# A decoder layer with product-key experts: one token block's search moved, gate tiles rounded earlier, one barrier taken out

## The chip, the cores and the metric

The kernel runs on one core of a Trainium2 chip, in one launch. The metric is the device time of that core in microseconds (us). The engines are TensorE (PE; PEld is its weight load), VectorE (DVE), ScalarE (ACT), GpSimd (POOL) and SyncE (SP). Each runs its own list of instructions in order, and they wait for each other by semaphores. DMA transfers are issued from SP's, ACT's and POOL's queues.

## The reference

One layer for 1,024 tokens of width 1,024, all in float32:

```
proj  = h @ w_in                     # attention q/k/v | recurrence f,i,q,g | memory q | 3 gates
mix   = (sum_g sigmoid(gate_g + b) * (branch_g @ w_branch_g)) @ w_out
h     = LN(alpha*h + mix)
q     = h @ w_q                      # 8 heads, 2 halves of 128
s1,i1 = top16(q1 . subkeys1); s2,i2 = top16(q2 . subkeys2)
top, pos = top16(s1 + s2 of all 256 pairs); idx = i1*128 + i2; gate = softmax(top)
out   = sum_e gate_e * gelu(h . u[idx_e]) * v[idx_e]       # 128 experts of 16,384 per token
h     = LN(alpha*h + out)
```

The three branches are a dilated sliding-window attention, a gated recurrence and a cross-attention to 256 memory tokens.

## The kernel before

Tokens go in two halves of 512 (`hf` 0 and 1), each of four blocks of 128. A half passes four stages: four heads of the branches (`PE_HEAD` and the loops over `NH`), the gated projection (`gated`, `mid_gates`, 8 steps of 6 weight tiles), the output projection with residual and norm (4 pairs of tiles) and the query projection (`query_tile`, `query`, 16 tiles). Between stages `cross(eng, n)` is a barrier: each of PE, ACT and DVE drains, adds one to `stage` and waits until all three have. SP and POOL wait on `stage` where they need it.

**Weight tiles.** A float32 product is made from three passes with rounded parts: high by high, low by high, high by low (lines 1082, 1085 and 1091). A tile of weights is rounded into `w_hi` by ACT (`weight_hi`, line 1530) and its rest is made into `w_lo` by POOL (`split_lo_only`, line 967). There are two buffers, taken in turn; `w_used` lets one be overwritten once PE has started the tile in the other. In the heads of the first half POOL makes both parts, in those of the second half both come back from DRAM. The first two gate tiles (`mid_hi(0, 0)` and `mid_hi(0, 1)`) are rounded by ACT after its last head; PE does them (`gated(0, 0)`, `gated(0, 1)`) ahead of the barrier `boundary(hf, 1)`. Behind it DVE splits the branches (lines 2306 and 2308).

**The experts of blocks 0 and 1.** In the second half DVE does expert dot products beside the layer's own work. POOL gathers rows of `u` by index into a ring of four (`u_rows`, line 988); a row's gather waits until the dot four rows back is done. The gathers stand in POOL's queue between the weight splits: in the query projection two behind each tile, 32 in all. DVE's `e_rows` (line 2089) multiplies a row by the token block and sums it; every fourth is followed by a copy (line 2093). The query projection has four groups of 8 rows; `e_gates` (line 2098) ends it.

**The searches.** A search (`topk`, lines 1971 to 2043) finds the top 16 for two expert heads of one block, so a block takes four. It needs four score matmuls of PE, and has four parts on DVE, each a chain of short instructions. Block 1 is searched beside the first half's query projection (`early_topk`, tiles named `_all`), blocks 0, 2 and 3 in the second half's heads, blocks 4 to 7 in the streamed stage (`late_topk`, tiles named `_own`).

**The streamed stage.** After the last barrier the whole table `v` passes through a ring of four tiles of 128 rows. There are nine streamed halves `p` of 64 tiles. In half `p` PE multiplies each tile with coefficients of blocks `p-1` and `p` (line 1420); from half 6, tile 32, by split parts (line 1453). Beside it DVE dots gathered `u` rows (`dot`, line 2429), a ring of seven, and in tiles 32 to 63 builds the coefficients of the next block (`hots`, `pair`). `turn(p + 1)` at tile 30 transposes the next block's indices and coefficients on PE (`transposes`, line 1099): it waits until DVE has done all dots of that block and multiplied the gates in. The next block's indices are loaded by `load_picks`. `searched(p)` says how many searches a half has, six tiles each:

```
return 3 if p < NB else 4 if p == NB else 0
```

So halves 0 to 3 have three, half 4 has four and half 5 none; NB is 4. `topk_at(p, i)` gives the search and part of a tile. Scores for a search are loaded by ACT's queue (`load_scores`: 256 KB of queries and 256 KB of keys).

## Time and profile before

| | us |
|---|---|
| median of 3 runs | 4026.82 (4024.84 to 5327.76) |
| the profiled execution | 4033.38 |
| its span, first to last instruction | 4031.1 |
| PE busy | 3658.6 (91%) |
| DVE busy | 2809.6 (70%) |
| POOL busy | 1577.5 (39%) |
| ACT busy | 1322.2 (33%) |

Busy time is the sum over an engine's instructions; a wait isn't busy. The mean granted clock of TensorE is 0.956 of full speed, and DMA moved 281 GB/s over the span. The streamed stage begins at about 1886 us. Matmul ends are modelled, so a busy PE isn't PE at its peak.

### The profile page before, as it was taken

The page shows a single profiled execution, that of the slowest core. Times are in us where ns is not written, and L with a number is a line of the kernel's source. Part 1 is how long each engine was busy: PE and PEld are TensorE (multiplying, and loading weights), DVE is VectorE, ACT ScalarE, POOL GpSimd, SP SyncE. Part 2 cuts the span into 40 slices and gives each one's busy share as a digit, 9 for nine tenths or more (in the row PEclk, how much of TensorE's full clock was granted, in tenths as well). Part 3 has the DMA queues.
Part 4 walks back from the last instruction along what each step waited for, and adds up shares of the span by engine and source line. Part 5 has one row for each costly group of instructions (what it writes and reads, how often), then busy time and mean ns, then how long its engine had stood idle before and what let it go on. Part 6 is the DMA issues. An engine that isn't in the chain of part 4 may idle for free.

```text
span 4031.1 us, 47164 instructions
## 1 busy us (share of the span) xinstructions
PE 3658.6 (91%) x14687; PEld 2513.0 (62%) x14687; DVE 2809.6 (70%) x5664; ACT 1322.2 (33%) x2671; POOL 1577.5 (39%) x1341
## 2 busy tenths in 40 slices
PE   6999989989889879868778999898998999999997
PEld 5878768777777768756534454453554545548874
DVE  1455542258778856665988888888889868868777
ACT  1333332222332332223533240330421403318445
POOL 2556534331222147656344443444544444520000
PEclk8999999989989989988899999999999999999999
DMA  7576633346767758769899999999999999984667
GB/s 242 197 237 219 218 92 99 107 149 229 237 210 240 227 167 262 265 234 335 276 400 405 393 396 368 388 387 393 389 378 369 408 401 398 393 332 143 204 213 256
DMA packets 506334, 1134.03 MB, mean 281 GB/s; under 512 B 41181, under 2 KB 250509, under 8 KB 505905
## 3 DMA queue, kind: packets, MB, share of 16 engines
q1 hardware_dynamic: 335120, 570.94, 40.7%
q0 software_dynamic: 147456, 536.94, 35.4%
q10 hardware_dynamic: 23584, 24.12, 1.7%
q8 instruction: 75, 1.23, 0.1%
q14 instruction: 99, 0.80, 0.1%
HBM read 1044.81 MB, written 89.41 MB: 281 GB/s over the span
## 4 chain that ended last, share of the span: by engine, by line
PE 33%; DVE 11%; DMA 6%; issue 2%; ACT 1%; POOL 0%; DVEq 0%; ACTq 0%
PE ps L1420 21%; PE ps L1453 6%; DVE u_ring L2429 5%; PE ps L1406 4%; DMA u_ring<-in_peer_u,pidx 4%; DMA v_ring<-in_peer_v 2%; DVE hot L2421 1%; DVE hot L2422 1%; DVE split_v L2482 1%; DMA score_in<-subkeys_t 0%; DVE got_own L2035 0%; PE h_up L1395 0%; DVE inds_own L1990 0%; DVE inds_own L1978 0%; ACT split_v L1877 0%
## 5 line engine op out<-in xcount | busy, mean ns | idle before, releaser
L1420 PE MATMUL ps<-v_ring,table 128*128 128x512 f32 x3072 | 1367.4, 596 | 19.4 <-DMA v_ring<-in_peer_v 19.2
L1023 POOL DMA_INDIRECT u_ring<-in_peer_u,pidx x800 | 775.1, 969 | 935.9 <-DVE coefe L2429 873.7
L2429 DVE CUSTOM_DVE_ANT_0 u_ring<-u_ring,h_up 128x1024 f32<-128x1024 f32 x800 | 948.0, 1217 | 138.0 <-DMA u_ring<-in_peer_u,pidx 122.1
L1420 PEld LDWEIGHTS ps<-v_ring,table 128*128 128x128 f32 x3072 | 570.1, 192 | 667.8 <-issue 632.4
L1082 PE MATMUL ps<-x_hi,w_hi 128*128 128x512 f32 x1280 | 517.0, 404 | 39.0 <-ACT w_hi L1530 23.6
L1085 PE MATMUL ps<-x_lo,w_hi 128*128 128x512 f32 x1280 | 507.1, 396 | 0.0
L1453 PE MATMUL ps<-split_v,split_c 128*128 128x512 f32 x1536 | 370.7, 395 | 20.9 <-DVE split_v L2482 18.8
L967 POOL TENSOR_TENSOR w_lo<-w_raw,w_hi 128x1024 fp32r<-128x1024 f32 x120 | 300.9, 2513 | 199.1 <-ACT w_hi L1530 193.3
L1406 PEld LDWEIGHTS ps<-hot,hot 128*128 128x128 f32 x2048 | 279.7, 201 | 150.8 <-issue 96.0
L1846 ACT ACTIVATE table<-ps 128x512 f32<-128x512 f32 (+3 forms) x256 | 230.8, 901 | 383.1 <-PE ps L1406 326.4
L1834 ACT ACTIVATE hot<-hot,by_slot 128x128 f32<-128x128 f32 x1024 | 322.0, 388 | 78.0 <-DVE hot L2421 68.3
L1453 PEld LDWEIGHTS ps<-split_v,split_c 128*128 128x128 f32 x1536 | 281.3, 188 | 97.6 <-DVE split_v L2482 35.2
L988 POOL DMA_INDIRECT e_ring<-in_peer_u,icole x224 | 229.6, 1025 | 277.1 <-DVE dotse L2089 198.6
L1406 PE MATMUL ps<-hot,hot 128*128 128x128 f32 x2048 | 289.7, 287 | 43.2 <-DVE hot L2422 18.5
L1091 PE MATMUL ps<-x_hi,w_lo 128*128 128x512 f32 x1280 | 317.3, 390 | 0.4 <-POOL w_lo L967 0.4
L1082 PEld LDWEIGHTS ps<-x_hi,w_hi 128*128 128x128 f32 x1280 | 246.3, 192 | 94.0 <-issue 13.5
L1085 PEld LDWEIGHTS ps<-x_lo,w_hi 128*128 128x128 f32 x1280 | 246.1, 192 | 52.5 <-issue 1.9
L1091 PEld LDWEIGHTS ps<-x_hi,w_lo 128*128 128x128 f32 x1280 | 239.7, 188 | 52.4 <-POOL w_lo L967 2.7
L2089 DVE CUSTOM_DVE_ANT_0 e_ring<-e_ring,h_up 128x1024 f32<-128x1024 f32 x128 | 155.0, 1220 | 130.1 <-DMA e_ring<-in_peer_u,icole 126.6
L2421 DVE TENSOR_TENSOR hot<-keys,by_slot 128x512 f32<-128x512 f32 x256 | 176.8, 691 | 96.2 <-PE ps L1406 71.4
L975 POOL TENSOR_TENSOR w_hi<-w_raw,zero 128x1024 fp32r<-128x1024 f32 x56 | 110.4, 1971 | 249.0 <-PE ps L1082 113.2
L1877 ACT ACTIVATE split_v<-v_ring 128x1024 fp32r<-128x1024 f32 x160 | 168.7, 1057 | 98.1 <-PE ps L1453 98.1
(327 smaller groups left out, 4462.5 us busy)
## 6 DMA issues: line engine op xcount, KB each, us to landing
v_ring<-in_peer_v SPq DMA_DIRECT2D x576, 512.0 KB
w_raw<-in_w_in SPq DMA_DIRECT2D x88, 512.0 KB
wh_d<-w_hi SPq DMA_DIRECT2D x56, 512.0 KB, 2.6
wl_d<-w_lo SPq DMA_DIRECT2D x56, 512.0 KB, 4.0
w_hi<-wh_d SPq DMA_DIRECT2D x56, 512.0 KB
w_lo<-wl_d SPq DMA_DIRECT2D x56, 512.0 KB
u_ring<-in_peer_u,pidx POOLq DMA_INDIRECT x800
raw_mid<-in_w_branch SPq DMA_DIRECT2D x48, 256.0 KB
```

What stands on the lines that cost most here:

```text
L967: pool.tensor_tensor(out=w_lo[b][:, 0:k, :], in0=raw[:, 0:k, :], in1=w_hi[b][:, 0:k, :].bitcast(F32), op=ALU.subtract).then_inc(w_split[b], 1)
L988: pool.indirect_dma_start(out=e_ring[:, s, :], out_offset=None, in_=u_tab, in_offset=bass.IndirectOffsetOnAxis(ap=icole[:, r, s:s + 1], ax ...
L1023: pool.indirect_dma_start(out=u_ring[:, slot_of(n, k), :], out_offset=None, in_=u_tab, in_offset=bass.IndirectOffsetOnAxis(ap=pidx[n % 2][ ...
L1082: first = pe.matmul(out, w_hi[b][:, k, :], hi[:, k, :], start=(k == 0), stop=False)
L1085: pe.matmul(out, w_hi[b][:, k, :], lo[:, k, :], start=False, stop=False)
L1091: last = pe.matmul(out, w_lo[b][:, k, :], hi[:, k, :], start=False, stop=(k == k_n - 1))
L1406: last = pe.matmul(build_bank(item)[:, P * m:P * m + P], hot2[sub % 2][:, m, :], hot1[sub % 2][:, m, :], start=True, stop=True)
L1420: last = pe.matmul(ps[2 * (n % 2) + c][:, :], table[:, row_of(n, i1), :], v_ring[:, j % V_TILES, HALF * c:HALF * c + HALF], start=(n == p ...
L1453: last = pe.matmul(ps[2 * (n % 2) + c][:, :], c_of[:, part_of(n, p, i), a, :], v[:, HALF * c:HALF * c + HALF], start=(n == p and i == 0 an ...
L1834: last = act.activation(hot1[sub % 2][:, m, :], hot1[sub % 2][:, m, :], ACT.Copy, scale=by_slot[:, 2, t0 + m:t0 + m + 1])
L1846: last = act.activation(table[:, r0:r0 + near, t0:t0 + TOK].rearrange("p i t -> p t i"), src[:, :, 0:near], ACT.Copy)
L2429: dve.tensor_tensor_reduce(out=u_ring[:, slot_of(n, k), :], in0=u_ring[:, slot_of(n, k), :], in1=h1_up[:, :, :].rearrange("p c n -> p (c n)"),
```

## The change

- ACT's head is now a function `act_head(h, last)`. The loop runs over three heads and the fourth is written out; in it `mid_hi(0, 0)` stands behind the copy `vn2` and `mid_hi(0, 1)` behind `values_out(2)`. Both halves.
- The barrier between gated and output projection is taken out in both halves. PE waits for ACT's last gates and DVE's last but one low part, and for the last only before the last high slice of the first output tile. SP loads residual and norm parameters after PE's last gated tile.
- In the second half's query projection three of block 4's four searches are done (`last_topk`), with the tiles of `early_topk`. Its loops on PE and DVE are written out, the rotated query tiles `qst_all` replace `qst`, and the keys are loaded there (1 MB).
- The streamed halves have 3, 2, 2, 2, 2, 2 searches. The last block's indices are loaded at tile 28 of half 5, not tile 48 of half 4. Some small tiles lie elsewhere.

```diff
+AHEAD = PH // 2 - 1
...
         def searched(p):
-            return 3 if p < NB else 4 if p == NB else 0
+            return 3 if p == 0 else 2 if p <= NB + 1 else 0
+
+        def first_part(p):
+            return AHEAD + sum(searched(k) for k in range(p))
...
             def load_ln(hf):
-                sp.wait_ge(stage, 3 * boundary(hf, 2))
+                sp.wait_ge(MP.sem, MP.after("B2", KD * hf + KD - 1))
...
-                    if hf == 0 and e == 2:
-                        sp.wait_ge(stage, 3 * boundary(0, 3))
+                    if e == 2:
+                        sp.wait_ge(stage, 3 * boundary(hf, 3))
                         sp.dma_start(skt_all[:, :, :], subkeys_t).then_inc(tk_in, 16)
...
-                        if p >= 1:
-                            sp.wait_ge(tk_out, late_stores(p))
...
-                        sp.wait_ge(turned, p + 2)
-                        load_picks(p + 3)
+                        if p + 3 < NBLK - 1:
+                            if p >= 1:
+                                sp.wait_ge(tk_out, late_stores(p))
+                            sp.wait_ge(turned, p + 2)
+                            load_picks(p + 3)
+                    if i == DOT_TILES and p == NB + 1:
+                        sp.wait_ge(tk_out, late_stores(NB))
+                        sp.wait_ge(turned, NBLK - 2)
+                        load_picks(NBLK - 1)
...
                 for k in range(k_n):
+                    if whole is not None and k == k_n - 1:
+                        pe.wait_ge(*whole)
...
-                cross(pe, boundary(hf, 2))
...
+                for t in range(2):
+                    pe.wait_ge(MA.sem, MA.after(f"s{t}", KD * hf + KD - 1))
+                pe.wait_ge(MV.sem, MV.after("lo", KD * hf + KD - 2))
+                out_pair(0, (MV.sem, MV.after("lo", KD * hf + KD - 1)))
+                with pe.Fori(1, KD // 2) as e:
+                    out_pair(e, None)
...
+                for q in range(PH // 2):
+                    for n in range(4):
+                        query_tile(2 * q + n // 2, n % 2)
+                        if q and n == 0:
+                            early_scores(q - 1)
...
                     spill(2)
+                    if last:
+                        mid_hi(0, 0)
                     p("p1p")
...
                     values_out(2)
+                    if last:
+                        mid_hi(0, 1)
                     v("md")
...
+                with act.Fori(0, NH - 1) as h:
+                    act_head(h, False)
+                act_head(NH - 1, True)
...
-                for t in range(2):
-                    mid_hi(0, t)
                 cross(act, boundary(hf, 1))
...
-                cross(act, boundary(hf, 2))
...
+            def last_topk(q, part):
+                topk(early, late_item(0, q), part, 4 + q % 2, late.idxu[:, 2 * TOPK * q:2 * TOPK * (q + 1)], late.gex[:, 2 * q:2 * q + 2, :])
...
-                cross(dve, boundary(hf, 2))
...
                 if hf == 1:
-                    with dve.Fori(0, PH // 2) as e:
+                    dve.wait_ge(e_out, 32)
+                    for e in range(PH // 2):
                         e_rows(0, E_PQ, G_PQ + E_PQ // E_ROWS * e, S_PQ + E_PQ * e, 0)
+                        if e:
+                            for part in range(4):
+                                last_topk(e - 1, part)
                     e_gates()
```

## Rows read from the trace of the kernel before

**Rows 1.** Timeline of PE at four stage ends: start, us, line, operation [idle before <- releaser].
```profile
541.66 0.76 PE L1082 MATMUL ps<-x_hi,w_hi 128*128 128x512 f32 x1 [7.77 <-DVE og L2130]
...
1466.34 0.77 PE L1082 MATMUL ps<-x_hi,w_hi 128*128 128x512 f32 x1 [9.75 <-ACT w_hi L1530]
...
751.37 0.54 PE L1082 MATMUL ps<-m_hi,w_hi 128*128 128x512 f32 x1 [4.36 <-ACT w_hi L1530]
...
1690.14 0.79 PE L1082 MATMUL ps<-m_hi,w_hi 128*128 128x512 f32 x1 [9.80 <-ACT w_hi L1530]
```

**Rows 2.** Windows: stretch, length, busy by engine (count), granted clock, DMA share, GB/s.
```profile
1788.00:1882.00 94.00, 89.48 (x384) 73.49 (x384) 43.66 (x73) 27.08 (x33) 70.02 (x56) 0.97 0.90 312
...
1690.00:1757.00 67.00, 55.21 (x224) 42.37 (x224) 42.56 (x74) 12.78 (x17) 49.74 (x47) 0.92 0.96 334
...
2696.00:2716.00 20.00, 20.00 (x54) 9.39 (x53) 16.80 (x60) 1.28 (x1) 5.63 (x6) 1.00 0.91 319
...
3258.00:3288.00 30.00, 30.00 (x72) 13.26 (x71) 19.54 (x33) 0.00 (x0) 14.95 (x16) 1.00 1.03 409
```

The engines stand in the order PE, PEld, DVE, ACT, POOL.

**Rows 3.** Timeline of SP and ACT in the first half's last head.
```profile
512.66 2.10 SPq L766 DMA_DIRECT2D w_raw<-in_w_in  x2
...
523.72 0.60 ACT L1587 ACTIVATE ptp<-ps 128x512 f32<-128x512 f32 x1 [2.09 <-PE ps L1099]
```

**Rows 4.** Timeline of DVE behind the barrier after the heads, both halves.
```profile
555.35 1.23 DVE L2306 CAST o_hi<-branch 128x2048 fp32r<-128x2048 f32 x1 [8.05 <-PEq L687]
...
1480.16 1.23 DVE L2306 CAST o_hi<-branch 128x2048 fp32r<-128x2048 f32 x1 [14.15 <-PEq L687]
```

**Rows 5.** Timeline of POOL and DVE around the second half's output projection.
```profile
1680.44 0.94 POOL L988 DMA_INDIRECT e_ring<-in_peer_u,icole  x1 [0.30 <-issue]
1690.17 2.38 POOL L967 TENSOR_TENSOR w_lo<-w_raw,w_hi 128x1024 fp32r<-128x1024 f32 x1 [8.79 <-ACT w_hi L1530]
...
1687.94 0.69 DVE L2337 TENSOR_TENSOR m_lo<-macc,m_hi 128x512 f32 x1
```

**Rows 6.** Groups by line, DVE, 1788 to 1882: busy, mean ns, idle before <- releasers.
```profile
L2089 DVE CUSTOM_DVE_ANT_0 e_ring<-e_ring,h_up 128x1024 f32<-128x1024 f32 x32 | 39.1, 1221 | 50.2 <-DMA e_ring<-in_peer_u,icole 49.7
```

**Rows 7.** Timeline of DVE and POOL, two searches in the first half's query projection.
```profile
901.68 0.89 DVE L1974 MAX8 vals_all<-h_up 128x8 f32<-128x128 f32 x4 [7.02 <-PE h_up L1128]
...
915.11 0.19 DVE L2039 SCALAR_TENSOR_TENSOR pidx_one<-got_all 128x32 uint32<-128x32 f32 x1
...
869.78 2.12 DVE L2039 SCALAR_TENSOR_TENSOR pidx_one<-got_all 128x32 uint32<-128x32 f32 x1
...
869.46 2.39 POOL L967 TENSOR_TENSOR w_lo<-w_raw,w_hi 128x1024 fp32r<-128x1024 f32 x1 [3.04 <-ACT w_hi L1530]
```

**Rows 8.** Timeline of DVE and POOL in the second half's query projection.
```profile
1796.40 1.22 DVE L2089 CUSTOM_DVE_ANT_0 e_ring<-e_ring,h_up 128x1024 f32<-128x1024 f32 x1 [9.88 <-DMA e_ring<-in_peer_u,icole]
...
1839.18 0.17 DVE L2093 COPY coefe<-dotse 128x4 f32 x1
...
1845.12 0.98 POOL L988 DMA_INDIRECT e_ring<-in_peer_u,icole  x1 [0.81 <-POOL icole L985]
...
1851.87 1.22 DVE L2089 CUSTOM_DVE_ANT_0 e_ring<-e_ring,h_up 128x1024 f32<-128x1024 f32 x1 [1.66 <-DMA e_ring<-in_peer_u,icole]
...
1881.75 0.29 DVE L2098 TENSOR_TENSOR coefe<-coefe,pgatee 128x128 f32<-128x128 f32 x1 [0.38 <-ACT coefe L1568]
```

**Rows 9.** Timeline of PE at the turns of streamed halves 1 to 5.
```profile
2274.48 0.38 PE L1099 MATMUL ps<-ident,key_f 128*128 128x128 f32 x2
...
2546.92 0.66 PE L1099 MATMUL ps<-ident,key_f 128*128 128x128 f32 x2 [15.11 <-DVE coefe L2434]
...
2816.25 0.66 PE L1099 MATMUL ps<-ident,key_f 128*128 128x128 f32 x2 [14.32 <-issue]
2816.70 0.42 PE L1099 MATMUL ps<-ident,coefe 128*128 128x128 f32 x1
...
3088.26 0.66 PE L1099 MATMUL ps<-ident,key_f 128*128 128x128 f32 x2 [15.95 <-issue]
...
3344.53 0.42 PE L1099 MATMUL ps<-ident,key_f 128*128 128x128 f32 x2 [3.25 <-issue]
```

More of the change, by code:

```diff
@@ L342, in layer @@
         res = at("res", [P, NB, D], offset=r_head)
[L343 to L344 removed]
+        r_top = top[0] + 8 * HALF
         ln_g = at("ln_g", [P, D], offset=r_ln)
@@ L1018, in _ @@
             pool.wait_ge(stage, 3 * boundary(1, 4))
+            for t in range(2):
+                pool.wait_ge(qp_out[t], 16 * PH * NHALF + 16)
             for n in range(1, NBLK):
@@ L1072, in _, with tile @@
             cross(pe, 1)
-            def tile(n, hi, lo, k_n, out, ready=False):
+            def tile(n, hi, lo, k_n, out, ready=False, whole=None):
                 b, m = n
@@ L1121, in early_scores @@
             def early_scores(q):
-                pe.wait_ge(tk_in, 16)
-                pe.wait_ge(QA.sem, QA.after("c1", 2 * q + 1))
+                first, block, bank = (0, 1, 6) if hf == 0 else (late_item(0, 0), 0, 4)
+                pe.wait_ge(tk_in, 16 * hf + 16)
+                pe.wait_ge(QA.sem, QA.after("c1", PH * hf + 2 * q + 1))
                 if q >= 2:
-                    pe.wait_ge(TK.sem, TK.after("rest", q - 2))
+                    pe.wait_ge(TK.sem, TK.after("rest", first + q - 2))
                 for n in range(4):
-                    last = pe.matmul(ps[6 + q % 2][:, P * n:P * n + P], qst_all[4 * (q % 2) + n][:, P:2 * P], skt_all[:, 4 * q + n, :], start=True, stop=True)
+                    last = pe.matmul(ps[bank + q % 2][:, P * n:P * n + P], qst_all[4 * (q % 2) + n][:, P * block:P * block + P], skt_all[:, 4 * q + n, :], start=True, stop=True)
                 last.then_inc(*TP.mark("s"))
@@ L1760, in mid_gates @@
                         mid_hi(j, 3 + b)
-                for t in range(2):
-                    mid_hi(0, t)
                 cross(act, boundary(hf, 1))
@@ L1793, in query @@
                     act.wait_ge(QP.sem, QP.after(f"Q{t}", it))
-                    rows = qst[t] if hf else qst_all[2 * (e % 4) + t]
-                    if hf == 0 and e >= 4:
-                        act.wait_ge(TP.sem, TP.after("s", e // 2 - 2))
+                    rows = qst_all[2 * (e % 4) + t]
+                    if e >= 4:
+                        act.wait_ge(TP.sem, TP.after("s", (late_item(0, 0) if hf else 0) + e // 2 - 2))
                     act.wait_ge(qp_out[t], 16 * it + 16)
```

50 lines of the change are left out of this document (20 added, 30 removed).

## The prediction, made before the changed kernel was run

> **What bounds the kernel now.** I read the windows first, to see which engine or transfer is full in a stretch; then the timeline where TensorE (PE) stood still; then groups by line; then single instructions. PE is busy for 91% of the span, so a part of the change pays only where PE or the end of a stage waits for it. Three places count.
>
> First, the ends of two stages in each half. After the last head PE waits 7.77 and 9.75 us for the first rounded weight tile, after the gated projection 4.36 and 9.80 us [rows 1]. Second, the second half's query projection: in 94 us VectorE (DVE) is busy 43.66, GpSimd (POOL) 70.02, DMA 0.90 of the time [rows 2]. DVE's other 50 us are waits for gathered expert rows [rows 6]. Third, the streamed stage. With no search in it PE goes from one turn to the next in 256.3 us; with three it takes 272.4 and 269.3, with four 272.0 (differences of start times in [rows 9]). DMA runs at 409 GB/s where there is no search, and at 319 where the first search holds DVE [rows 2].
>
> The sum is made against the profiled execution, 4033.4 us with a span of 4031.1; the median of the runs is 4026.8, so 6.6 lower. I take the same difference off both.
>
> **Step 1, two gate tiles rounded in the last head.** Removed: two ScalarE (ACT) roundings of 1.06 us behind the head, and the wait of PE for them. Added: the same two, earlier. The first goes where ACT waits 2.09 us for PE, here and at the same place of the second half [rows 3], so it is hidden; without that cover it would cost 1.1 us of a chain that PE follows. The second needs its buffer, which comes free as PE starts the first tile; it lies in front of ACT's wait for DVE, hidden too. POOL's two low parts move forward with them. The raw tiles are asked for 11 us before that place (512.66 against 523.72, [rows 3]), so I take them as landed. Both tiles then run from the end of the head, but the barrier behind them also waits for DVE. In the first half DVE waited 8.05 us at it and in the second 14.15 [rows 4]. The first half can thus give at most 8; there the tiles take some 10.9 us (sixteen of that kind take 89.5 us, so two 11.2, [rows 2]) after 533.9 (541.66 - 7.77, [rows 1]), so they end before DVE does: **-8**. In the second half PE needed 1480.1 - 1456.6 = 23.5 us [rows 1, 4] for a gap and two tiles, and needs 11: **-12.5**, within DVE's 14.15. Bounds: 0 and -22.
>
> **Step 2, the barrier between gated and output projection goes.** PE now starts the output tile and waits only before its last high slice for DVE's last low part. First half: 4.36 us of gap [rows 1]; the residual's load now starts with PE's last gated tile and not with the barrier, which gains a little less, so **-3.5** (0 to -4.4). Second half: it isn't PE that sets the pace (55.21 of 67 us busy, [rows 2]) but POOL, which splits a weight tile and then issues four gathers, in one queue, eight times. It had waited 8.79 us for the rounding behind the barrier [rows 5]. That wait goes; DVE's last low part ends at 1688.6, the first gather of the stage is then issued at about 1684.7 (1681.4, a split and the index copy) and lands some 7 us later, so DVE isn't late either: **-8.5** (-4, if PE's own stop for DVE counts, to -9.8).
>
> **Step 3, three searches beside the second half's query projection.** Added: 12 score matmuls on PE (12 x 0.42 us, the row at 2816.70 in [rows 9], 5 us), a 1 MB load of keys on SP's queue (some 3 us at 312 GB/s, [rows 2]), both beside the longer DVE, a wait of ACT for scores that are long made, and on DVE three searches. One ran from 901.68 to 915.4, 13.7 us, in the first half; another 15.7, since one instruction took 2.12 us and not 0.19 [rows 7]. I take 14.7. DVE's order is now: 8 rows; 8 rows, search; 8 rows, search; 8 rows, search. What is queued behind a search is the dots, and POOL waits for these: a gather into a ring of four needs the dot four rows back. POOL's splits of the weight tiles stand in the same queue, and PE waits for them.
> Worked out from the rows of before: the second group ends at 1839.35 [rows 8]. Search to 1854.1. Row 17 is dotted at 1855.4, and only then POOL can issue row 21, issued at 1845.12 before. It lands 6.75 us after its issue (1851.87 - 1845.12, [rows 8]), at 1862.2. With a split of 2.4 us [rows 7] between the pairs row 23 is issued at 1860.3 and dotted at 1867.0; the group ends at 1869.9. Search to 1884.6. Row 25 to 1885.9, row 29 issued there, the last split ends at 1890.5, row 31 issued at 1890.7, dotted at 1897.5; the group ends at 1900.2. Search to 1914.9, gate product 0.4: 1915.3, against 1882.1 [rows 8]: **+33**. PE's last tile ends at 1892.5 and isn't what is late. Nothing of the streamed stage may start, since the barrier behind it is kept.
> Lower bound: no wait of DVE but the first: from 1796.4 [rows 8], 43.7 us of rows [rows 2] and 44.1 us of searches end at 1884.2, with the gates +2.5. Upper bound: each search adds itself and a whole landing: 3 x (14.7 + 6.75) = +64. I take +33: it follows the queues row by row.
> The Trainium skill ("DMA: Bandwidth & Descriptors", Anatomy of one DMA) fits a GpSimd transfer at 2.0 us plus bytes over 436 GB/s, an estimate of 3.2 us for these 0.5 MB. The trace's 6.75 us is twice that, beside other traffic; by the rule the two exposed landings would make +26 of the +33.
>
> **Step 4, the streamed stage.** Searches per streamed half go from 3, 3, 3, 3, 4, 0 to 3, 2, 2, 2, 2, 2. Three cost (272.4 + 269.3) / 2 - 256.4 = 14.5 us, four 15.6. Two isn't in the trace: 7.8 if 15.6 is shared evenly, 13.4 if the third costs what the fourth did, 1.1; I take 10.6 in the middle. Half 0 is unchanged, and half 1's turn [rows 9] had no idle before it: 0. Halves 2, 3: -3.9 each; 4: -5.0; 5: +10.6, as it had none. Sum **-2** (-13 to +9). PE's wait at the turn, 15.11, 14.32 and 15.95 us against 3.25 [rows 9], is where this is seen. The last block's indices load later, at tile 28 of half 5; DVE wants them at tile 32, PE's four tiles cover it, else 2 or 3 us. The loops written out I cost at nothing: the first half's query stage is written out too, and PE runs in it without a gap over 1.5 us.
>
> **Sum.** -8 - 12.5 - 3.5 - 8.5 + 33 - 2 = -1.5. Profiled 4032; against the median **4025 us**.
>
> **Rivals.**
> A. *The searches fill DVE's idle.* For it: 50 us idle against 44 us of work [rows 6]. Against: that idle is a wait for the very gathers that a search holds back. Then step 3 is +3 and the total -32: 3995 us.
> B. *Slower: each search empties the gather ring.* One mechanism, in the query stage: POOL stands behind the search, then DVE behind the landing, three times: +64, total +29: 4056 us. It decides once step 3 is over 35 us. For it: POOL is busy 70 of 94 us and can't catch up; against: four rows are already in the ring.
> C. *DVE and POOL get in each other's way.* A DVE subtraction of a few numbers took 2.12 us, starting and ending with a 2.39 us split on POOL; the same took 0.19 alone [rows 7]. With two such meetings in each search it lasts 17.7 us: +9, total +8: 4034 us. The Trainium skill ("GPSIMD Engine Reference", Key points) says the two engines share their SBUF interfaces and contend when a DVE instruction has two SBUF inputs; a search has four such. By that rule the trace agrees, and it speaks against putting searches beside splits.
> D. *The change doesn't do what it says at the head*: raw tiles late or ACT's chain longer, so that the barrier stays where it was: +20.5, total +19: 4046 us.
>
> **How the numbers follow.** Forecast 50%, A 17%, B 10%, C 15%, D 8%. The range must leave out no more than 2 in 10: **3992 to 4048** holds the forecast with the bounds of step 4, A, C and D, and leaves B outside with the ends of the others. Two per cent is 80 us, about what a measurement of this kernel can tell from no change; no case reaches it, and even all lower bounds together, -22, -14, +3 and -13, give -46. Faster by over 2%: 3%, within: 94%, slower: 3%.
>
> **What would show it.** Step 1: PE's gaps of 7.77 and 9.75 us gone, the barrier 8 and 12.5 us earlier. Step 2: POOL's 8.79 us gone, PE stopping inside its first output tile in the second half. Step 3: DVE without long waits but for two near 7 us before the last groups, POOL waiting for dots, the stage 127 us and not 94. Step 4: PE's wait before turns near 11 us in all of the halves 2 to 5. I am wrong if the query stage grows by under 15 us or over 50, or if two searches cost a half as little as none.

## The result, and the profile after

| | before | after |
|---|---|---|
| median (10 runs each) | 4027.86 us | 4047.85 us (4040.65 to 4054.16) |
| profiled execution | 4033.38 us | 4051.59 us |
| its span | 4031.1 us | 4049.8 us |

The changed kernel takes 1.005 times as long, 95% interval 1.0037 to 1.0062: slower by 20 us, where no change was forecast. One execution of the kernel before took 5327.76 us and is left out of the ratio. The interval is some 5 us to either side, so the prediction's 80 us for what a measurement can tell from no change was far too wide. The changed kernel lies 23 us above the predicted time, just inside the range, and the time near it that a rival gave (D, 4046 us) is not the reason, as step 1 shows. The profiled executions differ by 18.2 us, and the comparisons of traces are between these two.

**Where it went, from stage to stage** (start-up was 0.5 us shorter, read from PE's first tile of the first head):

| | forecast | measured | read from |
|---|---|---|---|
| step 1, end of the heads, first half | -8 | -12 | DVE's cast behind the barrier, 555.35 to 542.71 |
| step 1, second half | -12.5 | -9.8 | the same, 1480.16 to 1455.80, less all that came earlier |
| step 2, first half | -3.5 | -2 | the barrier behind the output stage, 824.4 to 809.8 |
| step 2, second half | -8.5 | -0.4 | first query matmul, 1787.8 to 1763.0 |
| step 3, query projection, second half | +33 | +34.7 | first query matmul to the gate product |
| step 4, streamed stage | -2 | +8.8 | gate product (+9.9) to the end (+18.7) |

With the start-up the sum is the difference of the spans, +18.7, within the rounding. Step 3 came as worked out, and so did the sum of step 1. The 20 us lie in two places: the second half of step 2 gave nothing, and step 4 cost what it was to save.

**Step 1.** Timelines of the changed kernel: ACT in the first half's last head, PE behind it, and DVE at the two barriers that answer to [rows 4] (start, us, line, operation, idle before and its releaser):

```profile
520.46 1.06 ACT L1545 ACTIVATE w_hi<-w_raw 128x1024 fp32r<-128x1024 f32 x1 [1.01 <-issue]
...
544.02 0.47 PE L1096 MATMUL ps<-x_hi,w_hi 128*128 128x512 f32 x1 [1.40 <-ACT w_hi L1545]
...
542.71 1.23 DVE L2328 CAST o_hi<-branch 128x2048 fp32r<-128x2048 f32 x1 [1.03 <-PEq L690]
...
1455.80 1.23 DVE L2328 CAST o_hi<-branch 128x2048 fp32r<-128x2048 f32 x1 [1.21 <-PEq L690]
```

The first rounding stands inside ACT's head, PE's 7.77 us are gone, and DVE's waits of 8.05 and 14.15 us [rows 4] are down to 1.03 and 1.21. The barrier now comes when DVE comes. In the first half DVE comes earlier itself, which the forecast had capped it by. Before, the last three instructions of its head met two weight splits on POOL. First before, then after:

```profile
540.95 3.57 DVE L2130 TENSOR_TENSOR og<-og 128x512 f32<-128x512 f32 x2
...
541.59 5.15 POOL L967 TENSOR_TENSOR w_lo<-w_raw,w_hi 128x1024 fp32r<-128x1024 f32 x2 [29.94 <-ACT w_hi L1530]
...
544.75 2.54 DVE L2130 TENSOR_TENSOR branch<-og,msum 128x512 f32 x1 [0.23 <-DVE og L2130]
```

```profile
539.34 1.42 DVE L2152 TENSOR_TENSOR og<-og 128x512 f32<-128x512 f32 x2
...
540.99 0.69 DVE L2152 TENSOR_TENSOR branch<-og,msum 128x512 f32 x1 [0.23 <-DVE og L2152]
```

The same three instructions take 2.1 us and not 6.1, since the splits now run before them: that is the 4 us by which the first half beat its cap. In the second half DVE reached the barrier 3.2 us later than the earlier steps would have let it. Of these, 1.4 us are lost in its last instructions: it waits 2.05 us for ACT, which has a rounding in front, where it waited 1.55, and one instruction beside a split takes 1.62 us and not 0.69. So the second rounding wasn't wholly hidden.

**Step 2, second half.** POOL, DVE, PE and SP in the changed kernel around the start of the output stage, and then the first dot of that stage in the kernel before:

```profile
1655.73 0.37 SPq L818 DMA_DIRECT2D res<-in_x  x1
...
1656.74 2.42 POOL L977 TENSOR_TENSOR w_lo<-w_raw,w_hi 128x1024 fp32r<-128x1024 f32 x1
...
1662.56 1.22 DVE L2111 CUSTOM_DVE_ANT_0 e_ring<-e_ring,h_up 128x1024 f32<-128x1024 f32 x1 [2.34 <-DMA e_ring<-in_peer_u,icole]
1664.59 0.94 POOL L998 DMA_INDIRECT e_ring<-in_peer_u,icole  x1 [2.29 <-DVE dotse L2111]
1665.17 1.22 DVE L2111 CUSTOM_DVE_ANT_0 e_ring<-e_ring,h_up 128x1024 f32<-128x1024 f32 x1 [1.38 <-DMA e_ring<-in_peer_u,icole]
1667.20 0.93 POOL L998 DMA_INDIRECT e_ring<-in_peer_u,icole  x1 [1.68 <-DVE dotse L2111]
1667.23 0.70 DVE L2359 TENSOR_TENSOR m_lo<-macc,m_hi 128x512 f32 x1
...
1667.98 0.80 PE L1096 MATMUL ps<-m_hi,w_hi 128*128 128x512 f32 x1 [9.11 <-DVE m_lo L2359]
...
1675.42 1.22 DVE L2111 CUSTOM_DVE_ANT_0 e_ring<-e_ring,h_up 128x1024 f32<-128x1024 f32 x1 [7.49 <-DMA ln_b<-in_ln_b]
1676.83 0.18 POOL L995 COPY icole<-pidxe 128x4 uint32 x1 [6.29 <-DVE dotse L2111]
```

```profile
1701.18 1.22 DVE L2089 CUSTOM_DVE_ANT_0 e_ring<-e_ring,h_up 128x1024 f32<-128x1024 f32 x1 [12.54 <-DMA e_ring<-in_peer_u,icole]
```

POOL's wait of 8.79 us for the rounding [rows 5] is gone, as forecast, and its split runs at 1656.74 without one. But POOL then stands 2.29, 1.68 and 6.29 us for DVE's dots, DVE 2.34 and 1.38 us for gathers and 7.49 us for the residual load, and PE 9.11 us where it had stood 9.80 [rows 1]: 10.3 us of POOL's waits took the place of 8.8. (In the first half, PE stops for 1.94 us in its first output tile, which is most of why that half gave 2 us and not 3.5.)

**Step 3.** DVE and POOL around the first search in the query projection, then DVE's groups of the whole stage, which answer to [rows 6], and two gaps of PE:

```profile
1815.13 0.88 DVE L1995 MAX8 vals_all<-ps 128x8 f32<-128x128 f32 x4
...
1830.29 0.18 POOL L995 COPY icole<-pidxe 128x4 uint32 x1 [9.81 <-DVE dotse L2111]
...
1842.96 1.22 DVE L2111 CUSTOM_DVE_ANT_0 e_ring<-e_ring,h_up 128x1024 f32<-128x1024 f32 x1 [4.50 <-DMA e_ring<-in_peer_u,icole]
...
1848.60 0.89 DVE L1995 MAX8 vals_all<-ps 128x8 f32<-128x128 f32 x4
...
1863.63 0.18 POOL L995 COPY icole<-pidxe 128x4 uint32 x1 [11.03 <-DVE dotse L2111]
...
1877.97 0.89 DVE L1995 MAX8 vals_all<-ps 128x8 f32<-128x128 f32 x4
```

```profile
L2111 DVE CUSTOM_DVE_ANT_0 e_ring<-e_ring,h_up 128x1024 f32<-128x1024 f32 x32 | 38.2, 1218 | 40.2 <-DMA e_ring<-in_peer_u,icole 40.2
L2115 DVE COPY coefe<-dotse 128x4 f32<-128x4 f32 x8 | 10.4, 1300 | 0.3
```

```profile
1835.92 3.78 PE L1105 MATMUL ps<-x_hi,w_lo 128*128 128x512 f32 x8 [4.81 <-POOL w_lo L977]
...
1869.27 3.78 PE L1105 MATMUL ps<-x_hi,w_lo 128*128 128x512 f32 x8 [8.41 <-POOL w_lo L977]
```

Three searches of 13.7 us. Behind the first and the second POOL stands at the dots and PE then at POOL's split; behind the third no dots are left, and the stage ends with it. Of DVE's 50.2 us of idle only 10 were filled.

**Step 4.** PE at the turns of the streamed halves 1 to 6 of the changed kernel, which answer to [rows 9]:

```profile
2282.39 0.38 PE L1113 MATMUL ps<-ident,key_f 128*128 128x128 f32 x2
...
2552.70 0.66 PE L1113 MATMUL ps<-ident,key_f 128*128 128x128 f32 x2 [14.99 <-DVE coefe L2459]
...
2822.12 0.66 PE L1113 MATMUL ps<-ident,key_f 128*128 128x128 f32 x2 [14.91 <-DVE coefe L2459]
...
3090.27 0.66 PE L1113 MATMUL ps<-ident,key_f 128*128 128x128 f32 x2 [13.61 <-issue]
...
3361.19 0.66 PE L1113 MATMUL ps<-ident,key_f 128*128 128x128 f32 x2 [15.20 <-issue]
...
3618.85 0.66 PE L1113 MATMUL ps<-ident,key_f 128*128 128x128 f32 x2 [4.79 <-issue]
```

PE waits some 15 us with two searches in a half, as long as with three and four before [rows 9]. The differences of start times are 270.3, 269.4, 268.2, 270.9 and 257.7 us. Halves 2 to 5 together take 8.8 us more than before: against before half 2 gave 2.1 us, half 3 nothing and half 4 3.9, and half 5, which had no search, costs 14.7.

### The profile page after: what moved, and what is told of

The parts are those of the page before. It is cut to its first block, busy times and chain, and to the rows that moved or that the text cites. A ratio compares the mean times of both kernels' runs of the same rounds, so it can differ in the third digit from the quotient of the medians.

```text
span 4049.8 us, 46947 instructions
## 1 busy us (share of the span) xinstructions
PE 3659.5 (90%) x14687; PEld 2513.4 (62%) x14687; DVE 2824.6 (70%) x5664; ACT 1323.3 (33%) x2672; POOL 1573.2 (39%) x1341
## 4 chain that ended last, share of the span: by engine, by line
PE 41%; DVE 15%; DMA 11%; issue 7%; POOL 2%; ACT 1%; PEld 0%; DVEq 0%; POOLq 0%; PEldq 0%; SPq 0%; ACTq 0%
PE ps L1435 20%; DMA u_ring<-in_peer_u,pidx 7%; PE ps L1468 6%; PE ps L1421 4%; DVE u_ring L2454 4%; DMA e_ring<-in_peer_u,icole 2%; PE ps L1105 2%; DMA v_ring<-in_peer_v 2%; PE ps L1096 2%; PE ps L1099 2%; DVE e_ring L2111 1%; POOL e_ring L998 1%; DVE hot L2446 1%; DVE hot L2447 1%; PE h_up L1096 1%
## 5 line engine op out<-in xcount | busy, mean ns | idle before, releaser
L1435 PE MATMUL ps<-v_ring,table 128*128 128x512 f32 x3072 | 1365.0, 595 | 18.1 <-DMA v_ring<-in_peer_v 18.0
L1096 PE MATMUL ps<-x_hi,w_hi 128*128 128x512 f32 x1280 | 515.1, 402 | 21.5 <-ACT w_hi L1545 13.8
L1468 PE MATMUL ps<-split_v,split_c 128*128 128x512 f32 x1536 | 371.2, 396 | 21.5 <-DVE split_v L2507 18.7
L1105 PE MATMUL ps<-x_hi,w_lo 128*128 128x512 f32 x1280 | 320.9, 393 | 13.4 <-POOL w_lo L977 13.2
```

Of the source, the lines that this page charges most:

```text
L1096: first = pe.matmul(out, w_hi[b][:, k, :], hi[:, k, :], start=(k == 0), stop=False)
L1105: last = pe.matmul(out, w_lo[b][:, k, :], hi[:, k, :], start=False, stop=(k == k_n - 1))
L1435: last = pe.matmul(ps[2 * (n % 2) + c][:, :], table[:, row_of(n, i1), :], v_ring[:, j % V_TILES, HALF * c:HALF * c + HALF], start=(n == p ...
L1468: last = pe.matmul(ps[2 * (n % 2) + c][:, :], c_of[:, part_of(n, p, i), a, :], v[:, HALF * c:HALF * c + HALF], start=(n == p and i == 0 an ...
```

## The experiments

Unless it says otherwise a kernel is named by what differs from the changed one. Ratios are to the kernel before as it ran on the same chip; two kernels of different chips are compared by their ratios. The ratio of the changed kernel is 1.005.

**1 and 2. The steps apart.** Steps 1 and 2 alone, the searches back where they were:

```diff
-AHEAD = PH // 2 - 1
+AHEAD = 0
...
-            return 3 if p == 0 else 2 if p <= NB + 1 else 0
+            return (3, 3, 3, 3, 4, 0, 0, 0, 0)[p]
...
-                            for part in range(4):
-                                last_topk(e - 1, part)
```

> The changed kernel with no search in the second half's query projection and the streamed halves searched as before (3, 3, 3, 3, 4, 0): steps 1 and 2 alone. By the stage times of the two profiles steps 1 and 2 together gained 25 us and the searches lost 43, so theory Q (the loss is the searches' alone) expects 25 us under the kernel before, ratio 0.994, and a query stage of 94 us. Rival R (part of the loss comes with the written-out loops, the moved barrier or the later indices) expects less than 15 us gained.

The moved searches alone, with the roundings and the barrier back where they were:

```diff
-                act_head(NH - 1, True)
+                act_head(NH - 1, False)
...
+                for t in range(2):
+                    mid_hi(0, t)
                 cross(act, boundary(hf, 1))
...
-                for t in range(2):
-                    pe.wait_ge(MA.sem, MA.after(f"s{t}", KD * hf + KD - 1))
-                pe.wait_ge(MV.sem, MV.after("lo", KD * hf + KD - 2))
-                out_pair(0, (MV.sem, MV.after("lo", KD * hf + KD - 1)))
-                with pe.Fori(1, KD // 2) as e:
+                cross(pe, boundary(hf, 2))
+                with pe.Fori(0, KD // 2) as e:
```

> The changed kernel with steps 1 and 2 undone (gate tiles rounded behind the head, the barrier between gated and output projection back): the moved searches alone. If the parts add up (theory Q): 43 us over the kernel before, ratio 1.011; the query stage 128 us and turn to turn 268 to 271 us in halves 2 to 5. If steps 1 and 2 only shifted waits that the searches' part hides, it is as slow as the changed kernel, +20 us.

Measured: steps 1 and 2 alone 4002.81 us, ratio 0.9953 (0.994 to 0.9966), 18.5 us under the 4021.3 of the kernel before; the searches alone 4069.56, ratio 1.0121 (1.0104 to 1.0139), 48 us over it. So the change is a good part and a bad part. Their sum, +30 with an uncertainty of some 9 us, lies 10 over the +20 of both together: they add within their errors, and no more can be said. Experiment 1 lies between its two theories; of experiment 2's, the one by which the parts add holds.

**3. The residual's wait.** DVE waited once, ahead of the rows; here at each residual add (with steps 1 and 2 alone):

```diff
-                dve.wait_ge(res_in, 48 * (hf + 1))
                 def out_rows(first, last):
...
                             dve.wait_ge(OP.sem, OP.after(f"T{t}", it))
+                            apart(dve)
+                            dve.wait_ge(res_in, 48 * (hf + 1))
```

> e1 with one wait of DVE moved: for the residual and norm parameters (3 MB) not ahead of the output stage's first expert dots but ahead of each use of the residual. Theory L (in the changed kernel this wait ended at 1675.4 and held DVE's dots and so GpSimd's gathers and splits, which is why step 2 gave 0.5 us in the second half and not 8.5): 5 to 8 us under e1. Rival C (the 3 MB transfer itself, beside the gathers, sets the pace): within 2 us of e1.

Measured: 3999.82 us, ratio 0.9942 (0.9929 to 0.9955), 3.0 us under experiment 1: between the two theories. The trace says more. From DVE's cast behind the heads to the first query matmul it takes 307.7 us before, 307.2 after, 306.7 in experiment 1 and 303.9 here. The 7.49 us wait of DVE is gone, but PE still waits 9.11 us in its first output tile:

```profile
1662.86 0.79 PE L1096 MATMUL ps<-m_hi,w_hi 128*128 128x512 f32 x1 [9.11 <-DVE m_lo L2359]
```

**11. Is it PE's wait, then?** Experiment 3 with DVE's last low part ahead of the last two rows:

```diff
-                    if hf == 1:
-                        e_rows(6, 8, G_MID + E_MID // E_ROWS * j, E_MID * j, 0)
                     mh = m_hi[:, bass.ds(j, 1), :].rearrange("p a t -> p (a t)")
...
                     dve.tensor_tensor(out=ml, in0=macc[:, 0, :], in1=mh.bitcast(F32), op=ALU.subtract).then_inc(*MV.mark("lo"))
+                    if hf == 1:
+                        e_rows(6, 8, G_MID + E_MID // E_ROWS * j, E_MID * j, 0)
```

> The kernel with steps 1 and 2 alone and the residual waited for at each residual add (3999.8 us), but in a step of the second half's gated projection VectorE makes the low part first and then takes the last two expert rows. Both theories: PE's wait of 9.1 us inside its first output tile falls to 2 to 5 us, as the low part no longer stands behind rows whose gathers are late. Theory G (gathers and the ring set the end of the stage, as they did before the change, when PE's wait was 9.80 us): the query stage begins no more than 1.5 us earlier, the whole 3998 to 4001 us. Rival V (PE's wait carries through to the stage's end): 4 to 7 us earlier, 3993 to 3996 us.

Measured: 3999.64 us, ratio 0.993 (0.9917 to 0.9944). By the ratios, 0.993 against 0.9942 with intervals that overlap, the two theories can't be told apart; the traces decide. PE's stop is 6.4 us shorter, and 303.7 us go by to the first query matmul, where it was 303.9; PE stops later instead:

```profile
1657.02 0.79 PE L1096 MATMUL ps<-m_hi,w_hi 128*128 128x512 f32 x1 [2.69 <-DVE m_lo L2357]
...
1674.71 0.80 PE L1096 MATMUL ps<-m_hi,w_hi 128*128 128x512 f32 x1 [5.30 <-ACT w_hi L1545]
```

So theory G holds, as far as two single traces can show it: the end of this stage doesn't follow PE's wait.

Where POOL's lead went can be read from its splits in this stage, counted from DVE's cast behind the heads:

| POOL's split | before | changed kernel | experiment 3 |
|---|---|---|---|
| first | 210.0 | 200.9 | 200.7 |
| second | 218.1 | 212.4 | 212.0 |
| third | 228.4 | 226.7 | 225.0 |
| eighth | 269.4 | 268.9 | 265.7 |

The first split comes 9.1 us sooner than before, as forecast. 3.4 us of that are lost by the second, where POOL waits for the dots of the last two rows of the gated projection, and 4.0 by the third, behind DVE's 7.49 us wait. In experiment 3 that wait is gone, but POOL waits 2.16 us for the rounding of its third tile, and ACT 1.22 us for that tile's weights; 3.7 us of lead are left at the end.

**7. The order inside the query projection.** The same work, a part of a search behind each pair of rows:

```diff
-                        e_rows(0, E_PQ, G_PQ + E_PQ // E_ROWS * e, S_PQ + E_PQ * e, 0)
-                        if e:
-                            for part in range(4):
-                                last_topk(e - 1, part)
+                        for part in range(4):
+                            e_rows(2 * part, 2 * part + 2, G_PQ + E_PQ // E_ROWS * e, S_PQ + E_PQ * e, 0)
+                            if e:
+                                last_topk(e - 1, part)
```

> The changed kernel, but in the second half's query projection the four parts of a search stand between the pairs of gathered rows (two rows, a part, two rows, a part) and not all four behind eight rows. The same work in VectorE's queue in another order. Theory R (a search that stands as one piece empties the ring of gathered rows, and GpSimd with the weight splits behind the gathers waits for it): parts of 2 to 5 us fit under the 6.75 us of a gather, the stage is about 102 us long and not 130, the whole 25 to 30 us under the changed kernel, 4020 us. Rival T (VectorE's sum of work and GpSimd's sum is what fills the stage): within 5 us of the changed kernel, 4043 to 4050 us.

Measured: 4024.64 us, ratio 0.9998 (0.9987 to 1.0009), 0.52% or 21 us under the changed kernel, less than the 25 to 30 of theory R. The stage is 106.2 us long, not 128.9 (expected was 102). DVE's and POOL's groups of the stage:

```profile
L2111 DVE CUSTOM_DVE_ANT_0 e_ring<-e_ring,h_up 128x1024 f32<-128x1024 f32 x32 | 37.9, 1214 | 21.8 <-DMA e_ring<-in_peer_u,icole 21.8
...
L2115 DVE COPY coefe<-dotse 128x4 f32<-128x4 f32 x8 | 3.1, 389 | 0.3
```

```profile
L995 POOL COPY icole<-pidxe 128x4 uint32 x8 | 1.5, 186 | 5.0 <-DVE dotse L2111 5.0
```

In the changed kernel the last of these had waited 20.8 us for dots. Theory R holds in its direction, and rival T (within 5 us) does not: two thirds of step 3's price (34.7 us against 12) came from the search standing in one piece.

**4 and 5. Other counts of searches in a half**, both with steps 1 and 2 alone; first 4, 4, 4, 4, 0, 0, then 4, 4, 3, 3, 1, 1:

```diff
-            return (3, 3, 3, 3, 4, 0, 0, 0, 0)[p]
+            return (4, 4, 4, 4, 0, 0, 0, 0, 0)[p]
```

> e1 with the 16 searches of the streamed stage as 4, 4, 4, 4, 0, 0 and not 3, 3, 3, 3, 4, 0. Theory F (a half with two searches or more loses about 14 us whatever their number, one with none loses nothing): half 4 falls from 272 to 256 us from turn to turn, halves 2 and 3 stay within 3 us of 270: 12 to 15 us under e1, unless halves 0 and 1, which get one more, give some back. Theory P (each search costs its share, 3.9 to 4.8 us): halves 2 and 3 rise by 4 each, half 4 falls by 16: 4 to 8 us less under e1.

> Steps 1 and 2 alone, all sixteen searches in the streamed stage, spread over the streamed halves 0 to 5 as 4, 4, 3, 3, 1, 1. Two readings of what a search costs a streamed half. Theory K (a fixed price for any search at all, near 14 us, and little for each further one): the halves with one search are 10 us or more longer than one without (256.4 us), so about 267 to 270 us. Rival S (each search its share): with one search 260 to 263 us. Theory P (the first searches of a half are dear because they stand in tiles 0 to 11, where VectorE also does another block's residual and norm): one search costs more than half of what two cost, 7 to 10 us, so 263 to 267 us.

Measured: 4003.37 us, ratio 0.9957 (0.9942 to 0.9972), and 4020.68 us (one run). In experiment 4 half 4 without a search took 256.3 us and so saved 16.0 against experiment 1, but halves 2 and 3 took 276.0 and 272.9 us, 8 more together, and halves 0 and 1 together 11 more: nothing is left, and both theories missed. In experiment 5 the halves with one search took 267.0 and 267.1 us: one search costs 10.6. That is where the ranges of theories K and P meet. It rules out that each search costs its share, and leaves open whether it is the count or the place.

**8 and 12. The place in the half.** Two searches as in the changed kernel, in tiles 12 to 23 (the edit below), and in tiles 6 to 17 (the same with `- (p > 0)`):

```diff
-            slot, step = i // SEARCH_TILES, i % SEARCH_TILES - 2
+            slot, step = i // SEARCH_TILES - (4 - searched(p)) * (p > 0), i % SEARCH_TILES - 2
```

> The changed kernel, but the two searches of each of the streamed halves 1 to 5 stand in tiles 12 to 23 and not in 0 to 11. In tiles 1 to 8 VectorE also adds another block's residual and does its norm. Theory P (the two together overfill VectorE, the gathers stop, and with DMA full everywhere else at 409 GB/s the time lost is never regained): moved behind the norm a half with two searches costs 4 to 7 us over one without, not 13; halves 2 to 5 together 25 to 35 us shorter, 4013 to 4023 us. Rival K (a fixed price, from the score loads or the change of work itself): within 5 us of the changed kernel, 4043 to 4050 us.

> The changed kernel, the two searches of each of the streamed halves 1 to 5 in tiles 6 to 17. In tiles 0 to 11 such a half costs 13 us over one without a search, in 12 to 23 it costs 5.3. Theory P (the price is VectorE's debt from tiles 1 to 8: a wait of 4.5 us for the block's close, the residual and the norm, before and beside the first search): the debt from the close is partly paid by tile 8, so 6 to 9 us a half: halves 2 to 4 of 262 to 265 us, the whole 4018 to 4030 us. Rival (tiles 0 to 5 alone matter, all behind them cost the same): 5.3 us, 261 to 262 us, 4010 us.

Measured: 4009.45 us, ratio 0.996 (0.9944 to 0.9975), 0.9% or 36 us under the changed kernel, a little more than theory P expected; and 4034.19 us (one run), above the 4018 to 4030 expected. PE's waits at the turns of halves 2 and 3, in tiles 12 to 23 and then in 6 to 17 (half 3):

```profile
2535.54 0.66 PE L1113 MATMUL ps<-ident,key_f 128*128 128x128 f32 x2 [6.51 <-DVE coefe L2459]
...
2797.33 0.66 PE L1113 MATMUL ps<-ident,key_f 128*128 128x128 f32 x2 [6.46 <-DVE coefe L2459]
```

```profile
2813.53 0.66 PE L1113 MATMUL ps<-ident,key_f 128*128 128x128 f32 x2 [10.44 <-DVE coefe L2459]
```

What a half costs above one with no search (256.4 us), by the start times at the turns, means of the halves from 2 on without half 5 of experiments 8 and 9 (see experiment 9):

| searches in tiles | extra us | from |
|---|---|---|
| 0 to 5 | 10.6 | experiment 5 |
| 0 to 11 | 13.3 | the changed kernel |
| 6 to 17 | 8.6 | experiment 12 |
| 12 to 23 | 4.6 | experiment 8 |
| 0 to 17 (three) | 14.5 | before |
| 6 to 23 (three) | 9.6 | experiment 9 |
| 0 to 23 (four) | 15.6; 18.1 | before; experiment 4 |

Single halves with the same searches scatter: 254.9 to 258.5 us with none, 268.2 to 271.5 with two in tiles 0 to 11, 268.7 to 273.8 with three. So neighbours in this table, such as one search and two in the first tiles, can't be told apart for certain; 13.3 and 4.6 can. The fixed price is refuted: it hangs on the tiles. Tiles 6 to 17 lie between, at 263.6 to 266.1 us a half, so it isn't tiles 0 to 5 alone that matter. Why the first tiles are dear, the timeline of DVE shows (changed kernel, half 4):

```profile
2970.20 1.28 DVE L2467 SCALAR_TENSOR_TENSOR res<-res,ps 128x512 f32<-128x512 f32 x2 [4.52 <-PE ps L1435]
2976.35 0.89 DVE L1995 MAX8 vals_own<-ps 128x8 f32<-128x128 f32 x4 [2.58 <-PE ps L1449]
2984.73 1.28 DVE L2475 BATCH_NORM_STATS2 bst<-res 128x6 f32<-128x512 f32 x2
```

and the windows of the same 40 us, first in the changed kernel, then in experiment 8 (same half, the searches later), then before in half 5, which has none (columns as in [rows 2]):

```profile
2975.00:3015.00 40.00, 40.00 (x106) 18.70 (x105) 37.39 (x125) 2.77 (x3) 14.11 (x15) 1.00 0.95 342
...
3015.00:3088.00 73.00, 61.66 (x144) 26.98 (x142) 51.73 (x101) 0.00 (x0) 34.05 (x36) 0.94 1.01 397
```

```profile
2950.00:2990.00 40.00, 40.00 (x95) 17.76 (x94) 29.93 (x51) 0.20 (x1) 22.41 (x22) 1.00 1.01 396
...
2990.00:3057.00 67.00, 61.47 (x156) 27.88 (x155) 58.85 (x176) 1.59 (x2) 28.65 (x30) 0.97 1.03 406
```

```profile
3241.00:3281.00 40.00, 40.00 (x94) 17.67 (x93) 29.49 (x51) 1.49 (x2) 21.93 (x22) 1.00 1.00 392
```

A half has 128 rows and 64 tiles of half a megabyte to fetch, 100.7 MB; in 256.4 us that is 393 GB/s, and where it runs undisturbed the windows show 409 [rows 2]. So the streamed stage runs close to the limit of DMA, and what counts is how long DMA runs below that rate. PE has hardly more to spare, as the windows from turn to turn show, half 5 before without a search and half 4 of the changed kernel with two:

```profile
3088.26:3344.53 256.27, 253.02 (x776) 127.91 (x776) 196.84 (x333) 72.66 (x165) 122.56 (x130) 0.99 1.01 396
```

```profile
2822.12:3090.27 268.15, 254.54 (x791) 129.67 (x792) 219.69 (x445) 72.65 (x165) 122.06 (x129) 0.97 0.99 385
```

PE is busy for 253.0 of 256.3 us, so, as far as its modelled ends tell, no placing of searches could bring a half much under that. With searches PE's work is nearly the same, and the added time is its wait at the turn, where it needs DVE's dots of the last gathered rows. At the start of a half DVE waits 4.52 us for PE to close the block before last and 2.58 for the scores, then has that block's residual and norm. With a search among them DVE is busy for 37.39 of 40 us, POOL has 15 instructions and not 22, nearly all of them issues of a row, and DMA falls to 342 GB/s: 40 x (396 - 342) = 2.2 MB less, 5.3 us at full rate. Over the whole half the two windows give the account. 268.15 us at 385 GB/s are 103.2 MB, against 101.5 in the half without: 1.7 MB more, of which 1 MB is the score loads, 4.3 us at 396 GB/s. The lower mean rate adds 7.4 us, most of it the 5.3 above. Together that is the 11.9 us by which this half is longer. DMA runs near its full rate afterwards (397), so hardly anything is regained. With the same two searches in tiles 12 to 23 it runs at 396 in the first stretch, and at 406 where the searches stand. That it is the close, the residual and the norm beside the search that make the first tiles dear is read from these rows; none of the three was moved by itself.

**9. Good steps, searches late.** Steps 1 and 2 alone, with 3, 3, 3, 3, 2, 2 searches, the last ones ending with tile 23:

> Steps 1 and 2 alone, sixteen searches in the streamed stage as 3, 3, 3, 3, 2, 2, those of halves 1 to 5 in the last tiles before tile 24 (three: tiles 6 to 23, two: tiles 12 to 23). Against steps 1 and 2 alone with 3, 3, 3, 3, 4, 0 from tile 0 on (4002.8 us). Theory P: the halves 2 and 3 with three searches lose 4 to 6 us, half 4 loses 8 to 10, half 5 gains 4 to 7: sum 10 to 20 us less, 3983 to 3993 us. Rival K: halves 2, 3 and 4 the same, half 5 longer by 14: 4012 to 4018 us.

Measured: 3989.31 us, ratio 0.9914 (0.9893 to 0.9935). The expectation of theory P, 3983 to 3993 us, is met, and rival K's is not. Halves 2 and 3 with three took 266.4 and 265.6 us, half 4 261.4, half 5 266.8. That half 5 is dearer than half 4 has a cause of its own. It is seen in experiment 8 too, from which these rows of SP's queue and PE are:

```profile
3308.72 0.33 SPq L909 DMA_DIRECT2D pidx<-idx_d  x1
...
3309.75 1.85 SPq L924 DMA_DIRECT2D v_ring<-in_peer_v  x4
...
3313.50 2.08 PE L1435 MATMUL ps<-v_ring,table 128*128 128x512 f32 x2 [9.35 <-DMA v_ring<-in_peer_v]
```

SP waits for the last search's picks to be stored, the tiles of `v` are queued behind that wait, and PE stands 9.35 us without them (9.97 in experiment 9). The prediction had "else 2 or 3 us" for this load; in the changed kernel, where the searches end at tile 11, no such gap stands.

**10 and 13. All together.** The changed kernel with the edits of experiments 7, 3 and 11, the searches of halves 2 on in tiles 12 to 23, counts of 3, 4, 2, 2, 2, 0; then 3, 3, 2, 2, 2, 1:

```diff
-            slot, step = i // SEARCH_TILES, i % SEARCH_TILES - 2
+            slot, step = i // SEARCH_TILES - 2 * (p > 1), i % SEARCH_TILES - 2
```

> All together: the changed kernel with its search parts between pairs of rows in the query projection, the residual waited for at each residual add, the last expert rows of a gated step behind its low part, the streamed halves with 3, 4, 2, 2, 2, 0 searches, those of halves 2 to 4 in tiles 12 to 23. If the effects measured one by one add: 4024.6 (parts between pairs) - 27 (halves 2 to 4) - 15 (half 5 without a search) + 1 (half 1 with four) - 3 (residual) = about 3980 us, 3974 to 3986 us, 1.2% under the kernel before. Rival (they don't add, since a saved wait uncovers the next): 3990 us or more, no better than the searches late with steps 1 and 2 alone (3989.3 us).

> The best kernel so far (all measures together, 3, 4, 2, 2, 2, 0 searches, 3987.7 us) with one search taken from half 1 and put into half 5, in tiles 12 to 17. There halves 0 and 1 took 8.4 us more together with seven searches than with five (397.5 against 389.1 us); a search in tiles 12 to 23 costs some 2.7 us (5.3 for two). Forecast: halves 0 and 1 give back 3 to 5 us, half 5 costs 2 to 4 us, the whole 3984 to 3989 us. Rival (the last block's indices, loaded at tile 28, are waited for as where the search stood in tiles 18 to 23 and PE stood still 9.3 us): 3992 us or more.

Measured: 3987.66 us, ratio 0.99 (0.9884 to 0.9915), and 3986.71 us, ratio 0.9901 (0.9886 to 0.9916): 38 to 40 us under the kernel before, the fastest found, and no different from experiment 9 within the intervals. Experiment 10 missed its 3980: from the start of the streamed stage to the turn of half 1 it took 397.5 us with seven searches, 389.1 with five (experiment 7), where 1 us was expected. Experiment 13, with six, gave that and more back (386.9), but its one search in half 5 cost 6 us (262.4) and not 2 to 4. The same stretch with six searches scatters between 382 and 389 us in the kernel before and experiments 1, 3 and 11, so a few us there say little. The interleaved query projection costs 12 us, and with three searches fewer the streamed stage to the end is 12 us shorter in experiment 13 than in experiment 9, so whether they stand here or there no longer matters.

## Why the prediction was wrong, by its steps

**Step 1 was right** in its mechanism and its sum, -21.8 against -20.5; the halves missed by 4 us and 2.7 in opposite ways, which is luck. The cap of 8 in the first half held DVE's arrival fixed, and a part of that arrival was the collision of DVE with POOL's splits, which the change also moved. In the second half the roundings and splits put earlier cost DVE some of its lead, where the step had called them hidden.

**Step 2, second half, failed** (-8.5, bounds -4 to -9.8; measured -0.4). The step said that POOL's 8.79 us wait goes, and "DVE isn't late either". POOL's wait went. DVE was late, in two ways that follow from one edit of the change, the residual's load brought forward by the missing barrier. These 3 MB now start at 1655.73, while the last two rows of the gated projection are in flight. They were issued at 1654.53 and 1655.79 and dotted at 1662.56 and 1665.17, so the landings took 8.0 and 9.4 us; before, the same two took no more than 5.6 and 5.4. The low part was done 212.1 us after DVE's cast behind the heads, before 208.5. Then DVE waited 7.49 us for that load ahead of the first row of the stage; before, a wait of 12.54 us for a gather in the same place had hidden it. I had counted the load's start under step 2's first half, as a small loss of gain, and not asked what stood behind the wait for it on DVE's queue in the second. Experiment 3 takes the second of these away and gains 3 us; experiment 11 shows that PE's own stop is not among the causes. Of the other 5 us, 3.4 went while POOL waited for the dots of the two late rows, by the splits under experiment 11. The last 2 us or so are POOL's wait of 2.16 us for the rounding of its third tile in experiment 3; where that wait comes from stays open. That the load's traffic is what slowed the two gathers is read from the trace; no run has the barrier out and the load where it was.

**Step 3 was right** in size, +34.7 against +33, and in its queues: POOL standing 9.81 and 11.03 us behind searches, DVE then 4.50 us behind a landing. Experiment 7 confirms the reason, since the same work in another order costs 12. Rival A (DVE's idle gets filled) had the amount of idle right and the order wrong: neither of the two orders tried gave its +3, the better one gave +12. Two things the working did not have: PE's low passes waiting for the splits in the same queue (4.81 and 8.41 us), and the copies of DVE's results, 10.4 us for eight where they were 4.2. Searches of 13.7 us, where 14.7 was taken, gave back half of the second. Row by row the working held: the searches began 52, 86 and 115 us into the stage, where it had 52, 82 and 112. Rival B's own point, a stage over 35 us longer, was missed by a hair, but its price of +64 was far off.

**Step 4 failed** (-2, bounds -13 to +9; measured +8.8, at the upper bound). The sentence that failed is the choice "Two isn't in the trace: 7.8 if 15.6 is shared evenly, 13.4 if the third costs what the fourth did, 1.1; I take 10.6 in the middle." The upper end was the truth, 13.4, in the four halves 2 to 5 (13.3). The mid-point stood on no mechanism. Two rows that were there pointed to the upper end: three searches cost 14.5 and four 15.6, so the price was plainly not shared evenly, and DMA at 319 GB/s against 409 [rows 2] was where the *first* search stood. Read together they say that one search, in the dear place, pays nearly all. (The 13.4 rests on a third search costing what the fourth did, so that it came true so exactly is in part luck.) By 13.4 the step would have been -1.1, -1.1, -2.2, +13.4 = +9, and the forecast 4036.

**By the sum:** step 2 was off by +9.6, step 4 by +10.8, the rest by less than 1 together. "Step 4: PE's wait before turns near 11 us in all of the halves 2 to 5" was the line by which it could be seen to be wrong: it was 14 to 15. Rivals C and D didn't happen as such. C's three searches lasted 13.8, 13.7 and 13.7 us, no longer than the first half's. (Its count of DVE instructions with two SBUF inputs is short by one: the second and fourth part of a search have five tensor instructions of that kind.) That the measured time still fell inside the stated range, by 0.15 us, owes nothing to the working: the upper end was set by step 4's bound and rival D's 4046 us, and step 2's miss went beyond its own bounds.

## What to carry to other kernels

- When a kernel's long stage runs DMA near its top rate, price each insertion by the bytes DMA fails to move meanwhile, and keep it out of the stretch where the engine already has waits and work of its own. The place was worth 36 us here; the second, third and fourth search in a half cost some 1 to 3 us each, once one stood in the first tiles.
- A chain moved into idle time that is a wait for a ring of gathers is better cut to pieces shorter than the landing (6.75 us here): eight rows and then 13.7 us of search cost 35 us, two rows and then one of its four parts 12.
- When two counts of a thing are in the trace and a third is forecast, ask which one paid, and don't share evenly. And when a barrier goes, list every transfer that it had held back and who waits for it ahead of other work.

## What was not expected of the hardware

Copies of 128x4 numbers on DVE took 0.17 us alone [rows 8] and up to 2.33 us where they met a weight split on POOL. POOL and DVE in the changed query projection:

```profile
1866.86 2.36 POOL L977 TENSOR_TENSOR w_lo<-raw_pq,w_hi 128x1024 fp32r<-128x1024 f32 x1
1866.92 2.33 DVE L2115 COPY coefe<-dotse 128x4 f32<-128x4 f32 x1
```

The copy starts just behind the split's start and ends with it. Eight copies took 10.4 us in this kernel, 3.1 us in experiment 7. The Trainium skill ("GPSIMD Engine Reference", Key points) names two kinds of DVE instruction that contend with GpSimd for SBUF: those in a 2-port performance mode and those with two SBUF inputs. The head's combining instructions (6.1 us beside splits, 2.1 without) are of the second kind and agree with it. The copy has one input; whether it ran in a 2-port mode no trace here shows.

A gather of 0.5 MB landed in 6.75 us in the query projection before [rows 8]. At the end of the gated projection it took no more than 5.6 us before, and 8.0 to 9.4 us where a 3 MB load ran beside it.
